# Moving the split weights of the down projection to another byte offset modulo 256

## The reference

```python
def _conv_ffn(x, w_up, conv_w, conv_b, w_down):
    S = x.shape[1]
    h = x @ w_up                                  # 2048 -> 2 * 5632
    hp = jnp.pad(h, ((0, 0), (CONV_WIDTH - 1, 0), (0, 0)))
    hc = conv_b + sum(conv_w[kk] * hp[:, kk:kk + S] for kk in range(CONV_WIDTH))
    gate = hc[..., :D_FF]
    up = hc[..., D_FF:]
    return (jax.nn.silu(gate) * up) @ w_down      # 5632 -> 2048

for i in range(DEPTH):                            # DEPTH = 2
    h = x @ (pool_w_in[j] if i % 2 == 0 else diff_w_in[j])
    ...                                           # token mixer, and attention into 256 memory tokens
    y = jnp.concatenate([mix, mem_o], axis=-1) @ w_out[i]
    x = _layernorm(DEEPNORM_ALPHA * x + y, ln1_g[i], ln1_b[i])
    f = _conv_ffn(x, ffn_w_up[i], ffn_conv_w[i], ffn_conv_b[i], ffn_w_down[i])
    x = _layernorm(DEEPNORM_ALPHA * x + f, ln2_g[i], ln2_b[i])
```

## The kernel before

| operand | part | before | after |
|---|---|---|---|
| ring `w_hi`, `w_lo`, all but the down projection | stationary or moving | 192 (192, 192) | 192 (448, 192) |
| ring in the down projection | moving | 192 | 128 |
| `act` | stationary, down | 192 | 192 |
| `pair_x` | stationary, down | 128 | 192 |
| `xT` (`ffn_xT`) | moving, up and pool input | 128 (384) | 128 (384) |
| `memT` | moving for keys, stationary for values | 128 (128) | 128 (128) |
| `tokens_xT` | stationary | 192 | 192 |
| `held`, `next` | moving | 192 | 192 |
| `up_pair_w`: four granules of the up projections | stationary | 224 | 224 |

## Time and profile before

### The profile page before, as it was taken

How to read it: one execution, slowest core, us unless ns; L and a number is a source line. 1 busy time by engine, 2 the same in 40 slices (tenths; PEclk the granted TensorE clock), 3 DMA queues, 4 the chain that set the end, 5 groups by cost and what they waited for, 6 DMA issues and landing times.

```text
span 2085.5 us, 38897 instructions
## 1 busy us (share of the span) xinstructions
PE 2079.5 (100%) x14538; PEld 1919.0 (92%) x14538; DVE 1527.7 (73%) x2708; ACT 1224.7 (59%) x2220; POOL 2.7 (0%) x12
## 2 busy tenths in 40 slices
PE   9999999999999999999999999999999999999999
PEld 8999889999999998888888888899999999988887
DVE  6767777767666669988756558667766677688888
ACT  5645566556555555665656666566555565555654
POOL 0000000000000000000000000000000000000000
PEclk9999999999999999999999999999999999999999
DMA  9655666555655655556544454745655555565554
GB/s 345 237 176 167 211 218 215 186 200 181 201 195 188 200 177 206 190 194 222 193 171 156 168 182 163 257 156 192 201 191 192 197 185 198 170 215 182 202 202 162
DMA packets 201631, 408.97 MB, mean 196 GB/s; under 512 B 7616, under 2 KB 9152, under 8 KB 200768
## 3 DMA queue, kind: packets, MB, share of 16 engines
q1 hardware_dynamic: 201392, 407.45, 57.3%
q10 hardware_dynamic: 144, 0.26, 0.0%
HBM read 404.53 MB, written 3.15 MB: 195 GB/s over the span
## 4 chain that ended last, share of the span: by engine, by line
PE 98%; DVE 1%; DMA 0%; SPq 0%; ACT 0%; issue 0%
PE acc L1810 32%; PE acc L1808 32%; PE acc L1809 32%; PE acc L2139 0%; DMA head_first<-in_first 0%; PE acc L2113 0%; PE acc L1921 0%; PE acc L2163 0%; PE acc L1914 0%; PE acc L2171 0%; DVE x_tok L1779 0%; PE acc L2009 0%; PE acc L1977 0%; PE acc L1997 0%; SPq L539 0%; DVE x_tok L1784 0%
## 5 line engine op out<-in xcount | busy, mean ns | idle before, releaser
L1078 DVE TENSOR_TENSOR w_lo<-raw,w_hi 128x512 fp32r<-128x512 f32 x1330 | 881.5, 688 | 397.3 <-ACT w_hi L638 393.0
L638 ACT ACTIVATE w_hi<-raw 128x512 fp32r<-128x512 f32 x1330 | 811.4, 630 | 543.7 <-PE acc L1810 528.3
L1808 PE MATMUL acc<-ffn_xT,w_hi 128*128 128x256 f32 x2920 | 806.7, 276 | 0.0
L1809 PE MATMUL acc<-ffn_xT,w_hi 128*128 128x256 f32 x2920 | 806.2, 276 | 0.0
L1810 PE MATMUL acc<-ffn_xT,w_lo 128*128 128x256 f32 x2920 | 806.2, 276 | 0.0
L1809 PEld LDWEIGHTS acc<-ffn_xT,w_hi 128*128 128x128 f32 x2920 | 548.4, 188 | 0.1
L1808 PEld LDWEIGHTS acc<-ffn_xT,w_hi 128*128 128x128 f32 x2920 | 548.2, 188 | 0.1
L1810 PEld LDWEIGHTS acc<-ffn_xT,w_lo 128*128 128x128 f32 x2920 | 548.1, 188 | 0.0
L1809 PE MATMUL acc<-w_lo,ffn_act 128*128 128x512 f32 (+1 forms) x642 | 235.4, 367 | 0.0
L1808 PE MATMUL acc<-w_hi,ffn_act 128*128 128x512 f32 (+1 forms) x642 | 235.3, 366 | 0.0
L1810 PE MATMUL acc<-w_hi,ffn_act 128*128 128x512 f32 (+1 forms) x642 | 235.1, 366 | 0.0
(11 more groups left out here) (306 smaller groups left out, 1963.4 us busy)
## 6 DMA issues: line engine op xcount, KB each, us to landing
raw<-in_ffn_w_up SPq DMA_DIRECT2D x172, 1024.0 KB, 5.0
raw<-in_ffn_w_down SPq DMA_DIRECT2D x88, 1024.0 KB, 5.1
raw<-in_diff_w_in SPq DMA_DIRECT2D x38, 1024.0 KB, 5.7
raw<-in_w_out SPq DMA_DIRECT2D x32, 1024.0 KB, 5.1
raw<-in_pool_w_in SPq DMA_DIRECT2D x16, 1024.0 KB, 5.1
raw<-in_mem_w_kv SPq DMA_DIRECT2D x12, 1024.0 KB, 12.5
next_from_raw<-in_ffn_w_up SPq DMA_DIRECT2D x4, 1024.0 KB, 10.2
head_first<-in_first SPq DMA_DIRECT2D x5, 768.0 KB, 11.4
```

What stands on the lines that cost most here:

```text
L638: nc.scalar.activation(hi, raw_place(st, c, k, j), ACT.Copy).then_inc(hi_made, 1)
L1078: nc.vector.tensor_tensor(lo, raw_place(st, c, k, j), hi.bitcast(F32), ALU.subtract).then_inc(lo_made, 1)
L1808: pe.matmul(out, w[0], x[0], start=start, stop=False, skip_group_check=True)
L1809: pe.matmul(out, w[0], x[1], start=False, stop=False, skip_group_check=True)
```

## The change

A second view of the ring's stretch is made for the down projection, 64 bytes lower than the ring: `down_hi`, `down_lo` (offset 128 modulo 256). Gaps of 256 bytes go ahead of both halves of the ring, which leaves all later tensors where they were modulo 256 (512 bytes further on). `pair_x` gets a margin of 64 bytes. Since the shifted slot overlaps the ring slot that the up projection has just filled, the first granule of each down projection is put into `first_hi`, `first_lo` over `gb`, and ACT waits there for `gb_free`. No instruction is added, removed or moved.

```diff
+SPLIT_GAP = 64
...
     raw = sb("raw", [P, SLOTS, PIECE * CHUNK])
-    w_hi = sb("w_hi", [P, HALVES * PIECE, CHUNK], F32R)
-    w_lo = sb("w_lo", [P, HALVES * PIECE, CHUNK], F32R)
-    x_tok = sb("x_tok", [P, TT, D])
...
+    ring, gap = [P, HALVES * PIECE, CHUNK], [P, SPLIT_GAP]
+    _, down_hi, _, down_lo = region("down", [("margin", [P, SPLIT_GAP - SPLIT_MARGIN], F32), ("w_hi", ring, F32R), ("gap", gap, F32), ("w_lo", ring, F32R)])
+    sb("hi_gap", gap)
+    w_hi = sb("w_hi", ring, F32R)
+    sb("lo_gap", gap)
+    w_lo = sb("w_lo", ring, F32R)
+    x_tok = sb("x_tok", [P, TT, D])
+
     kv_lo, = region("conv", [("kv_lo", [P, 4, 512], F32R)])
     conv = sb("conv", [P, 2, 2, 512])
+    first_hi, first_lo = region("down_first", [(x, [P, CHUNK], F32R) for x in ("hi", "lo")])
     gb = sb("gb", [P, 2, CHUNK])
...
-    pair_x, = region("pairs", [("x", [P, len(PAIR_SUM), len(PAIRED), 2, 2, P], F32R)])
+    _, pair_x = region("pairs", [margin, ("x", [P, len(PAIR_SUM), len(PAIRED), 2, 2, P], F32R)])
...
+    def is_first(st, c, k, j):
+
+        return st in s_down and isinstance(c, int) and (c, k, j) == (0, 0, 0)
...
             hi, lo = split_apart[st][0:2]
             return hi[:, j % 2, :], lo[:, j % 2, :]
+        if is_first(st, c, k, j):
+            return first_hi[:, :], first_lo[:, :]
         at = st.split_at(c, k, j)
+        if st in s_down:
+            return down_hi[:, at, :], down_lo[:, at, :]
         return w_hi[:, at, 0:st.width], w_lo[:, at, 0:st.width]
...
                 free = s_out[s_up.index(st)].used(0)
+            if is_first(st, c, k, j):
+                act_e.wait_ge(gb_free, 4 * s_down.index(st) + 2 + 1)
```

## The result

The changed kernel takes 2094.76 us (median of 8 runs, 2093.28 to 2095.91) against 2087.74 us for the kernel before: ratio 1.0033, 95% interval 1.0024 to 1.0043. It is 7.0 us slower. The kernel before spreads more than the 0.04% given at the start: 21 later executions lie between 2086.56 and 2089.68 us. The forecast was 2085.3 us with a range up to 2090.5. The sign and the range were both wrong; the time lies in the stretch that rival B gave, 2092.8 to 2095.3.

What follows compares the result with a forecast made beforehand. PE bounds the kernel: number of matmuls times the distance between their starts. Only the paired pieces' `act` matmuls gain, -2.5 us, all other terms 0: 2087.84 - 2.5 = 2085.3 us, range 2082.5 to 2090.5.

Steps and rivals of the forecast that it cites:

- rival B: Down projection's 512-column matmuls become slower, 231.7 ns or the full 6.7 ns more: 2092.8 to 2095.3 us; chance 0.11.
- Term 1: 414 256-column `act` matmuls of paired pieces, moving offset 192 to 128: from 119.4 to 113.3 ns, -2.5 us.
- Term 2: 552 `pairs_x` matmuls, from stationary 128, moving 192 to the exchanged pair: both at 113.3 ns, 0.
- Term 3: 1500 512-column down projection matmuls, moving offset 192 to 128: taken as 0, bounds -3 to +10 us.
- Term 4: First 512-column matmuls after each paired piece, 0.7 us lost in changeovers: taken as 0, bounds -0.7 to 0.
- Term 5: All else keeps its offset modulo 256 and moves 256 or 512 bytes, 8760 up projection matmuls included: 0.
- Terms 6 and 7: ACT's `gb_free` wait at a down projection's first granule, and ACT and DVE at other addresses: 0 each.

Runs made afterwards that it cites:

- spare128: hybrid with the spare place of each paired piece's first granule at 128 modulo 256 instead of 192; 2088.68 us against 2087.68, ratio 1.0006.
- after: The changed kernel itself, as profiled after the change, against the kernel before; 2094.76 us against 2087.74, ratio 1.0033.
- act128: Kernel before with only act moved to 128 modulo 256, ring left at 192 (stationary 128, moving 192); one execution, 2089.73 us beside 2087.68.
- m192: Changed kernel with the shifted view 256 instead of 64 bytes below the ring, moving weights at 192 again; 2091.42 us against 2087.94, ratio 1.0017.
- all128: Kernel before with every operand of the large products at 128 modulo 256; one execution, 2149.93 us beside 2087.07.
- hybrid: Changed kernel with the shifted view for paired pieces alone, each one's first granule over gb, ring at 192 for the others; 2085.70 us against 2087.94, ratio 0.9989.
- m0: Changed kernel with the view 192 instead of 64 bytes below the ring, moving weights at 0 modulo 256; one execution, 2093.88 us beside 2087.94.

## Why the prediction was wrong

**Term 1** held: the 414 `act` matmuls went to 113.3 ns, 18 of them in 2.04 us. Counted by their mean, 119.6 to 113.6 with a slow one at each changeover, that is -2.4 us instead of -2.5. But it held with luck. The prediction took 113.3 ns as the distance of this pair, and the pair has a second one, 117.8, that `spare128` ran into. The trace of the kernel before showed it already: in the pool input projection, with `ffn_xT` and `w_hi` as in the up projection, 47 matmuls from 128.54 to 134.08 take 5.54 / 47 = 117.9 ns.

**Term 2** held, with the same luck: `pairs_x` stayed at 113.3 ns.

**Term 3** failed, and it alone. The 1500 matmuls of 512 columns were put at 0 and rose by 6.2 ns in the mean (227.1 to 233.3), +9.2 us. The choice was between two nearest rows, and I took the one with the same offsets at half the width over the one with the same width at exchanged offsets. Neither was right: the first is contradicted by `after` itself, the second by `act128` against `after`. Width and side both change the answer. The profile held a warning that I listed and did not weigh: the earlier trace rows already had the two widths rank equal offsets in opposite order, so a row of one width was no evidence for the other. The upper bound of the term was right. Rival B gave 2092.8 with the distance of the six matmuls after a paired piece, and 2095.3 with the full 6.7 ns of the 256-column ones; the measurement, 2094.76, is near the second. It deserved more than 0.11, and the range should have reached to it, since a term without a row carried 1.5 us for each ns.

**Term 4** does not count any more, since all 512-column matmuls are as slow as those few were.

**Term 5** held: `m192`, with the same gaps and the same 448 modulo 512, shows the old distances, and the up projections took no more time.

**Terms 6 and 7** held: ACT did not wait for `gb_free`, and DVE kept 1.2 us of idle time in a period.

Sum of the terms with their measured sizes: -2.4 + 9.2 = +6.8 us. The two down projections grew by 6.85 us in the trace and the median by 7.0. The rule of two independent read ports and of a PE that never waits on anyone (the Trainium skill, "SBUF — State Buffer", "Who interferes with whom"), read as the prediction reads it, would have given 0. The traces disagree with it so read: placement alone was worth +7.0 us here, and 62.9 us in `all128`. The 518 cycles, about 216 ns, that "TensorE: Matmul & The Clock Gate", "Back-to-back issue gap" (the Trainium skill) gives for an isolated matmul of 512 columns were not reached at any pair of the table; the smallest steady value there was 226.7 ns.

What stays open: why the pairs rank as they do, and what picks the distance where a pair has two. The runs show what the distances are, not which part of the chip delays the stream. A matmul without its weight load, which might show that, was not tried.

## What to carry to other kernels

In a stream in which every matmul has its own weight load, place the stationary and the moving operand deliberately, and measure each width at its own pair: of the pairs tried here, equal modulo 256 was best for 512 columns, 128 against 192, either way round, for 256 columns, and a price at one width says nothing on the other. When one term of a sum has no row of its own and is multiplied by thousands, put its dearest neighbour inside the range. After any such edit look at the distances of the untouched stages too: the same pair can have two distances, and which one a stage has can change the time by as much as the edit.

## What was not expected of the hardware

At 256 columns with stationary 192 and moving 128 there are two steady distances, 113.3 and 117.8 ns, and what comes ahead can decide for a whole paired piece: six matmuls at equal offsets in `hybrid` led to the faster one, a direct change from 512 columns at equal offsets in `spare128` to the slower one. In `m0` and `act128` 432 matmuls of stages that the edits leave alone had 117.8 where eleven other traces have 113.4. With stationary 128 and moving 192 at 512 columns one and the same program showed 233.3 ns in one execution and 228.9 in another. With equal offsets only one distance was seen for each width, 120.0 and 226.7 ns, at 192 and at 128 alike.
